# Softmax left undivided in two branches of a decoder trunk: gate over sum, spread by TensorE, multiplied into the head's output

## The reference, cut to what matters

```python
p2 = jax.nn.softmax(s2.reshape(B, Qb, Hk, G, n_top * NSA_SEL_LEN), axis=-1).reshape(s2.shape)
o_s = jnp.einsum('bqhgnl,bqhnld->bqhgd', p2.astype(vsel.dtype), vsel)
...
o_w = banded_attention(q, k_w, v_w, pos, NSA_WINDOW, slopes)
return gates[..., 0:1] * o_c + gates[..., 1:2] * o_s + gates[..., 2:3] * o_w
```

## Time and profile before

| | |
|---|---|
| median of 3 runs | 2594.37 us (2593.79 to 2594.88) |
| the profiled execution's own time | 2596.74 us |
| its span | 2594.9 us |
| PE busy | 94% of the span |
| DVE busy | 59% |
| ACT busy | 44% |
| granted TensorE clock over the span | 0.971 |

### The profile page before, as it was taken

How to read it: one execution, slowest core, us unless ns; L and a number is a source line. 1 busy time by engine, 2 the same in 40 slices (tenths; PEclk the granted TensorE clock), 3 DMA queues, 4 the chain that set the end, 5 groups by cost and what they waited for, 6 DMA issues and landing times.

```text
span 2594.9 us, 37597 instructions
## 1 busy us (share of the span) xinstructions
PE 2437.7 (94%) x13276; PEld 2007.8 (77%) x13276; DVE 1518.7 (59%) x3235; ACT 1136.4 (44%) x2267; POOL 135.0 (5%) x194
## 2 busy tenths in 40 slices
PE   6998899999999889999989998999999988999998
PEld 4887787788877678888868877878878776788886
DVE  5668776772775555552275786767447566455422
ACT  4456564643544532222243564646346445222222
POOL 3000000000002100000010000000000112000000
PEclk8999999999999889999999999999999989999999
DMA  4321122123124113333322211221321420233332
GB/s 110 98 90 34 50 62 61 58 65 97 42 89 123 30 53 96 95 95 95 87 74 74 82 33 57 66 66 50 81 74 50 130 65 25 81 97 97 94 97 69
DMA packets 343959, 193.96 MB, mean 75 GB/s; under 512 B 29825, under 2 KB 339206, under 8 KB 343174
## 3 DMA queue, kind: packets, MB, share of 16 engines
q1 hardware_dynamic: 340512, 178.02, 24.0%
q0 software_dynamic: 2224, 13.67, 1.5%
q10 hardware_dynamic: 1078, 0.36, 0.1%
HBM read 184.69 MB, written 7.34 MB: 74 GB/s over the span
## 4 chain that ended last, share of the span: by engine, by line
PE 81%; DVE 10%; ACT 4%; issue 4%; POOL 1%; DVEq 0%; POOLq 0%; ACTq 0%
PE acc L1257 63%; PE o_acc L1257 5%; PE turn L1461 3%; PE scores L1257 3%; ACT w_hi L797 2%; DVE w_lo L1788 1%; PE turn L1257 1%; DVE ring L2065 1%; PE scores L1446 1%; DVE ring L1873 1%; DVE p_lo L1906 1%; PE scores L1447 1%; DVE trunk L1879 1%; PE scores L1506 1%; PE scores L1325 1%
## 5 line engine op out<-in xcount | busy, mean ns | idle before, releaser
L1788 DVE TENSOR_TENSOR w_lo<-w_f,w_hi 128x1024 fp32r<-128x1024 f32 x336 | 412.0, 1226 | 563.4 <-ACT w_hi L797 563.1
L1257 PE MATMUL acc<-h_hi,w_hi 128*128 128x512 f32 x1680 | 670.7, 399 | 21.3 <-DVE w_lo L1788 9.3
L1257 PE MATMUL acc<-h_lo,w_hi 128*128 128x512 f32 x1680 | 664.7, 396 | 0.0
L1257 PE MATMUL acc<-h_hi,w_lo 128*128 128x512 f32 x1680 | 663.9, 395 | 0.0
L797 ACT ACTIVATE w_hi<-w_f 128x1024 fp32r<-128x1024 f32 x336 | 353.8, 1053 | 295.7 <-PE acc L1257 268.3
L1257 PEld LDWEIGHTS acc<-h_hi,w_hi 128*128 128x128 f32 x1680 | 321.1, 191 | 85.7 <-DVE w_lo L1788 11.0
L1257 PEld LDWEIGHTS acc<-h_hi,w_lo 128*128 128x128 f32 x1680 | 320.4, 191 | 66.8
L1257 PEld LDWEIGHTS acc<-h_lo,w_hi 128*128 128x128 f32 x1680 | 321.2, 191 | 59.8
L853 ACT ACTIVATE p_hi<-turn 128x128 fp32r<-128x128 f32 (+3 forms) x356 | 149.6, 420 | 270.7 <-PE turn L1461 268.5
L1906 DVE TENSOR_TENSOR p_lo<-turn,p_hi 128x128 fp32r<-128x128 f32 (+3 forms) x356 | 165.7, 466 | 73.2 <-ACT p_hi L853 72.6
L941 ACT ACTIVATE ring<-ring,neg_max 128x128 f32<-128x128 f32 (+2 forms) x352 | 188.9, 537 | 38.0 <-DVE neg_max L2065 37.2
(11 more groups left out here) (351 smaller groups left out, 3844.5 us busy)
## 6 DMA issues: line engine op xcount, KB each, us to landing
w_f<-in_ffn_w_in_dram SPq DMA_DIRECT2D x88, 512.0 KB, 3.8
w_f<-in_w_gate_dram SPq DMA_DIRECT2D x64, 512.0 KB, 4.0
w_f<-in_w_in_dram SPq DMA_DIRECT2D x62, 512.0 KB, 3.9
w_f<-in_w_branch_dram SPq DMA_DIRECT2D x32, 512.0 KB, 3.4
w_f<-in_ffn_w_out_dram SPq DMA_DIRECT2D x32, 512.0 KB, 4.0
w_f<-in_w_out_dram SPq DMA_DIRECT2D x16, 512.0 KB, 4.2
w_f<-in_ffn_w_out_dram SPq DMA_DIRECT2D x16, 384.0 KB, 3.4
x_spill<-trunk POOLq DMA_DIRECT2D x2, 2048.0 KB, 6.8
```

The costliest lines, as they stand in the source:

```text
L1257: ins = nc.tensor.matmul(dst, a, b, start=(n == 0 and not added), stop=(n == count - 1))
L1788: nc.vector.tensor_tensor(w_lo[:, u % 2, :], w_f32[:, u % 2, :], w_hi[:, u % 2, :].bitcast(F32), ALU.subtract).then_inc(w_ready, 1)
```

## The change

The exp results of SEL and WIN are turned and multiplied with the values as they are. Once a head, when its four row sums are there, DVE makes gate/sum for the 4x128 queries and splits it (`head_scale`, four instructions on 128x4). PE spreads it over 64 partitions with 8 matmuls against the identity (`spread_scale`), into one more use of the `turn` banks. ACT copies that bank to `square_sum` (`scale_rows`). DVE multiplies `o_acc` with it into `pair_next` (`head_scaled`) and adds the product to `y_nsa` (`out`, one turn of the loop later than before). The other passes keep their division.

```diff
-TURNS = [("v_cmp", 1), ("cmp", 2), ("v_sel", 1), ("sel", 32), ("v_win", 1), ("win", 32),
+TURNS = [("v_cmp", 1), ("cmp", 2), ("v_sel", 1), ("sel", 40), ("v_win", 1), ("win", 40),
...
+    def slot(self, s):
+        return s + max((s - 2) // NT, 0) * (self.gate is not None)
+    def spread_slot(self, h):
+        return min(5 * h + 6, 5 * self.heads - 1)
...
# ScalarE
+                def scale_rows(h):
+                    at = ps.spread_slot(h)
+                    turn_high_part(l, ps.name, 0, at, square_sum[h % 2 * HD:(h % 2 + 1) * HD, :],
+                                   turn[(TB[ps.name] + at) % 2][0:HD, :])
...
+                    if ps.gate is not None and 6 <= s and s % NT == 2:
+                        scale_rows(s // NT - 1)
...
-                    late = 8 if ps is WIN else 6
+                    late = 9 if ps is WIN else 6
...
# TensorE
                 def turn_probs(s):
-                    pe.wait_ge(divided, st + (s + 1))
+                    if ps.gate is None:
+                        pe.wait_ge(divided, st + (s + 1))
+                    else:
+                        wait_apart(pe, exped, st + (s + 1))
...
+                def spread_scale(h):
+                    bank = turn_bank(l, ps.name, 0, ps.spread_slot(h))
+                    pe.wait_ge(gate_split, (2 * l + (ps is WIN)) * H + h + 1)
+                    for i in range(NT):
+                        for m, part in enumerate((gate_hi, gate_lo)):
+                            ins = nc.tensor.matmul(bank[0:HD, i * P:(i + 1) * P],
+                                                   part[:, h % 2, i:i + 1].to_broadcast([P, HD]), ident_r[:, :],
+                                                   start=(m == 0), stop=(m == 1))
+                    ins.then_inc(turned, 1)
...
+                    if ps.gate is not None and s >= 6 and s % NT == 2:
+                        spread_scale(s // NT - 1)
+                if ps.gate is not None:
+                    spread_scale(ps.heads - 1)
...
# VectorE
-                    dve.wait_ge(turned, l * NTN + (TB[ps.name] + max(s - RING + CREDIT, 0) + 1))
+                    free = ps.slot(s - RING) + CREDIT if s >= RING else max(s - RING + CREDIT, 0)
+                    dve.wait_ge(turned, l * NTN + (TB[ps.name] + free + 1))
...
+                def head_scale(h):
+                    done = (2 * l + (ps is WIN)) * H + h + 1
+                    own = gate_over[:, h % 2, :]
+                    dve.wait_ge(exped, st + (4 * h + 4))
+                    nc.vector.reciprocal(over_sum[:, :], row_sum[:, h % 2 * NT:(h % 2 + 1) * NT]).then_inc(inverted, 1)
+                    dve.wait_ge(inverted, st + (h + 1))
+                    nc.vector.tensor_tensor(own, over_sum[:, :], coef[:, ps.gate, :, h], ALU.mult).then_inc(over_gated, 1)
+                    dve.wait_ge(over_gated, done)
+                    nc.vector.tensor_copy(gate_hi[:, h % 2, :], own).then_inc(gate_high, 1)
+                    dve.wait_ge(gate_high, done)
+                    nc.vector.tensor_tensor(gate_lo[:, h % 2, :], own, gate_hi[:, h % 2, :].bitcast(F32),
+                                            ALU.subtract).then_inc(gate_split, 1)
+                def head_scaled(h):
+                    rows, t = slice(h % 2 * HD, (h % 2 + 1) * HD), TB[ps.name] + ps.spread_slot(h)
+                    dve.wait_ge(turn_high, l * NTN + (t + 1))
+                    dve.wait_ge(applied, st + (4 * h + 6))
+                    dve.wait_ge(head_done, l * NHD + (HB[ps.name] + h + 1))
+                    nc.vector.tensor_tensor(pair_next[rows, :], o_acc[h % 2][0:HD, :], square_sum[rows, :],
+                                            ALU.mult).then_inc(turn_ready, 1)
...
                 def out(h):
-                    dve.wait_ge(applied, st + (4 * h + 6))
+                    dve.wait_ge(turn_ready, l * NTN + (TB[ps.name] + ps.spread_slot(h) + 3))
-                    nc.vector.tensor_tensor(dst, src, dst, ALU.add).then_inc(head_done, 1)
+                    nc.vector.tensor_tensor(dst, pair_next[rows, :], dst, ALU.add).then_inc(head_done, 1)
...
                     if 1 <= s <= ps.steps:
-                        divide(s - 1)
+                        if ps.gate is None:
+                            divide(s - 1)
+                        elif s % NT == 0:
+                            head_scale(s // NT - 1)
...
-                    if s >= 7 and (s - 7) % 4 == 0 and (s - 7) // 4 < ps.heads:
-                        out((s - 7) // 4)
-                    if ps is WIN and s >= 13 and (s - 13) % 8 == 0:
-                        nsa_rest((s - 13) // 8)
+                    if ps.gate is not None and s >= 7 and (s - 7) % 4 == 0 and (s - 7) // 4 < ps.heads:
+                        head_scaled((s - 7) // 4)
+                    late = 7 if ps.gate is None else 8
+                    if s >= late and (s - late) % 4 == 0 and (s - late) // 4 < ps.heads:
+                        out((s - late) // 4)
+                    if ps is WIN and s >= 14 and (s - 14) % 8 == 0:
+                        nsa_rest((s - 14) // 8)
```

More of the change, by code:

```diff
@@ L286, in build @@
         neg_max = sb("neg_max", [P, 4])
-        row_sum = sb("row_sum", [P, 4])
+        row_sum = sb("row_sum", [P, 8])
+        gate_over = sb("gate_over", [P, 2, NT])
+        gate_hi = sb("gate_hi", [P, 2, NT], F32R)
+        gate_lo = sb("gate_lo", [P, 2, NT], F32R)
         sink_exp = sb("sink_exp", [P, 4])
@@ L384, in build @@
         divided = sem("divided")
+        over_gated = sem("over_gated")
+        gate_high = sem("gate_high")
+        gate_split = sem("gate_split")
         out_high = sem("out_high")
@@ L934, in probabilities @@
                 def probabilities(s):
+                    many = 4 if ps.gate is None else 8
                     h, i = divmod(s, NT)
@@ L949, in high @@
                         act.wait_ge(cmp_applied, 2 * KVH * (l + 1))
-                    turn_high_part(l, ps.name, 0, s, p_hi[0:rows, s % 2, 0:n * P],
-                                   turn[(TB[ps.name] + s) % 2][0:rows, 0:n * P])
+                    at = ps.slot(s)
+                    turn_high_part(l, ps.name, 0, at, p_hi[0:rows, s % 2, 0:n * P],
+                                   turn[(TB[ps.name] + at) % 2][0:rows, 0:n * P])
+                def scale_rows(h):
+                    at = ps.spread_slot(h)
+                    turn_high_part(l, ps.name, 0, at, square_sum[h % 2 * HD:(h % 2 + 1) * HD, :],
+                                   turn[(TB[ps.name] + at) % 2][0:HD, :])
                 def out_high_part(h):
@@ L1457, in turn_probs @@
                     n, w = ps.tiles(s % NT)
-                    bank = turn_bank(l, ps.name, 0, s)
-                    pe.wait_ge(divided, st + (s + 1))
+                    bank = turn_bank(l, ps.name, 0, ps.slot(s))
+                    if ps.gate is None:
+                        pe.wait_ge(divided, st + (s + 1))
+                    else:
+                        wait_apart(pe, exped, st + (s + 1))
                     for t in range(n):
@@ L1473, in apply @@
                         pe.wait_ge(cmp_out, 2 * KVH * (l + 1))
-                    pe.wait_ge(turn_ready, l * NTN + (TB[ps.name] + s + 3))
+                    pe.wait_ge(turn_ready, l * NTN + (TB[ps.name] + ps.slot(s) + 3))
                     for t in range(n):
@@ L2082, in divide @@
                     p = ring[:, s % RING, 0:ps.keys(i)[1]]
-                    if ps.gate is None:
-                        nc.vector.tensor_scalar(p, p, over_sum[:, c], None, ALU.mult).then_inc(divided, 1)
-                    else:
-                        nc.vector.tensor_scalar(p, p, over_sum[:, c], coef[:, ps.gate, i, h:h + 1], ALU.mult,
-                                                ALU.mult).then_inc(divided, 1)
+                    nc.vector.tensor_scalar(p, p, over_sum[:, c], None, ALU.mult).then_inc(divided, 1)
+                def head_scale(h):
[17 more added lines that the diff above has]
+                                            ALU.mult).then_inc(turn_ready, 1)
                 def out(h):
@@ L2117, in attend @@
                     value_turns(l, *values)
-                for s in range(ps.steps + 6):
+                for s in range(ps.steps + (6 if ps.gate is None else 7)):
                     if s < ps.steps:
@@ L2125, in attend @@
                         n, rows = ps.tiles(t % NT)
-                        turn_rest(l, ps.name, 0, t, p_lo[0:rows, t % 2, 0:n * P],
-                                  turn[(TB[ps.name] + t) % 2][0:rows, 0:n * P], p_hi[0:rows, t % 2, 0:n * P])
+                        at = ps.slot(t)
+                        turn_rest(l, ps.name, 0, at, p_lo[0:rows, t % 2, 0:n * P],
+                                  turn[(TB[ps.name] + at) % 2][0:rows, 0:n * P], p_hi[0:rows, t % 2, 0:n * P])
                     for n, (name, k) in enumerate(ps.filler):
@@ L2133, in attend @@
                             stage(n)
-                    if s >= 7 and (s - 7) % 4 == 0 and (s - 7) // 4 < ps.heads:
```

(8 more changed lines are left out.)

2 lines of the change are left out of this document (1 added, 1 removed).

## The result

The changed kernel takes 2618.2 us (median of 4 runs, 2617.45 to 2619.61), the kernel before 2594.62 us in the same session (4 runs, 2593.79 to 2600.55). The ratio is 1.0087, with a 95% interval of 1.0072 to 1.0101: slower by 0.9%, 23.6 us. The prediction said 2615 and 2601 to 2627.

What follows compares the result with a forecast made beforehand. PE was taken as the bound. A layer: SEL 2.85, SEL to WIN 2.7, WIN 2.65, behind WIN 1.4, clock 0.75, together 10.35; two layers +20.7 on 2594.4, about 2615 us, range 2601 to 2627.

Steps and rivals of the forecast that it cites:

- The sum by periods: Inside SEL and WIN: split and plain periods grow, the first period gains; +2.85 in SEL, +2.65 in WIN a layer.
- WIN's last period: End of WIN's pass: the last head's spread falls before the filler ends and adds 0.48 us.
- the price of the earlier trace: Spread on PE: upper bound from a 128-wide scale's spread, 0.14 us a matmul, 1.1 us a head, 36 us.
- The 81 ns of the Trainium skill: Spread on PE: about 81 ns a matmul would make 0.65 us a head, 5 us more over the kernel.
- The boundary: From SEL to WIN: last spread and ACT's copy precede WIN's weight split; PE stands 3.6 us or more; +2.7.
- The end of WIN: Behind WIN: ACT's copy and `head_scaled` join the chain to `y_lo`, latency 1.65, tail shorter by 0.6; +1.4 to 1.5.
- The clock: Start of WIN: PE's stand may drop it to 1.2 GHz, losing up to 1.7 us; one in two, 0.75 a layer.
- the rival in which VectorE's relief wins: SEL, WIN and tails: DVE was the bound, stalls go, 11 us a layer; less 15.4 for the spread, 2588 us; 7%.
- the 0.35 of the prediction: Last turns of SEL, without filler: the last values product ends 0.35 us earlier than before.
- gains and spread cancel: Rival, SEL and WIN: split periods lose their stall (-9.8), the tails keep half of theirs: 2597 us; 9%.
- ACT's copy delays the exp: SEL and WIN: the copy's 0.59 us a head lies in ACT's idle time; otherwise exps late, stall grows as much.

Runs made afterwards that it cites:

- WIN's keys first: Changed kernel with SEL's last head finished (copy, product, add) behind WIN's first weight split and keys: 2611.66 us, ratio 1.0057.
- the double spread: Changed kernel with sixteen spread matmuls a head instead of eight, the same values computed twice: 2633.07 us, ratio 1.0129.
- the run with the later add: Changed kernel with the head's output add and what follows it one more turn later, no longer between `w_lo` and the bias: 2608.94 us, ratio 1.0042.
- both moves: Changed kernel with output add one turn later and SEL's last head finished behind WIN's keys: 2599.07 us, ratio 1.0010.
- the last kernel: Changed kernel with output add later, SEL's last head behind WIN's keys, spread as four turns, last spread ahead of last values product: 2595.1 us, ratio 0.9998.
- half the spread: Changed kernel with four spread matmuls a head instead of eight, low part of gate over sum left out: 2613.84 us, ratio 1.0054.
- the kernel with both moves and the last spread early: Changed kernel with add later, SEL's last head behind WIN's keys, each pass's last spread ahead of its last values product: 2602.83 us, ratio 1.0017.

## Why the prediction was right

The forecast was 2615 us, +20.7; measured 2618.2, +23.6, and +20.2 in the stages that the change touches. Slower was given 0.84.

*The sum by periods held in SEL, and in WIN only with the clock's help.* SEL +2.85 and WIN +2.65 a layer were forecast; +2.81 and +2.92 were measured between the first and last bias. But WIN's 2.92 holds the low clock, which the forecast counted by itself: with the clock at 1.00 (WIN's keys first) WIN takes 59.10 us, +1.5. The single periods came at 8.58 and 9.15 to 9.42 (forecast 8.55 and 9.2) in SEL and 7.71 and 8.7 (7.6 and 8.9) in WIN; too much was forecast above all for WIN's last period, to which 0.48 was added and which did not grow (7.81 us between the bias rows of 512 keys before, 7.71 after). The spread's 0.48 us a head was right (0.059 a matmul), and the double spread shows that each further matmul counts whole; the price of the earlier trace rows was not paid. The 81 ns of the Trainium skill (TensorE: Matmul & The Clock Gate, Back-to-back issue gap) is not what this stream took.

*The boundary held:* first scores behind 3.72 and 3.70 us of standing (3.6 forecast). The stage grew by 2.44 for 2.7. *The end of WIN* was too small in the sum: the wait came (1.80 us), and the stage grew by 2.0 for 1.4. *The clock* was given one in two and fell in both layers; it costs 1.3 to 1.4 us a layer by the runs, for 0.75 in the sum. So the 10.35 a layer against 10.1 measured is partly luck: WIN 1.1 too much and the boundary 0.3, the clock and the end of WIN 0.6 too little each.

*What VectorE gives and takes was mis-sized on both sides, and the total hides it.* I let the missing division give back 0.3 to 0.45 in a split period and little elsewhere, and so put the removal at 6 to 7 us a layer when it went to the test. It was worth 8.8, against the 11 of the rival in which VectorE's relief wins. Between the ends of `p_lo` of 512 keys, split periods of WIN went from 8.35 to 7.70 and plain ones from 7.26 to 7.08; in SEL the split ones from 8.85 to 8.38, and the plain ones not at all (7.79 to 7.77), as forecast. Most of the rest came at the ends of the passes, which have no filler: SEL's last period gave 0.8 to 1.1, WIN's 1.4, and the boundary 1.3, for the 0.35 of the prediction. What took it away again is the other half of VectorE's exchange, 6.9 us a layer for four small operations, product and add. I had priced the add at 0.6 in each of six split periods, 3.6 a layer, and that is what these periods show; the 3.3 in WIN's plain periods, in the last period of each pass and at the end of WIN were not in the sum. The exchange leaves 1.9 us a layer of gain, for VectorE's 22.7 us less of busy time.

*The sum of the causes,* a layer: the divisions gone -8.8; VectorE's new work +6.9; spread, copy and clock +12.0, of which the issue of 128 spread matmuls is 7.7. The run with the double spread shows the 7.7 for the second eight; for the first eight the periods of SEL and the timeline show the same price. The other 4.3 lie at the ends and in the clock: the boundary (9.42 to 13.11, 2.7 beyond the 0.96 of its two spreads), the end of WIN (36.31 to 37.89, 0.6 beyond its two) and WIN (56.58 to 60.53, 1.1 beyond its six). That is +10.1. This is one order of adding the parts up, and the parts are not independent: with the add one turn later SEL's split periods are as long as its plain ones, with the spread in them.

*The rivals.* That the relief wins failed not for lack of a stall but because its new operations stand at worse places than the old ones: the place of the add alone is 3 to 4 us a layer, as the run with the later add shows, some 2.9 of it in the split periods. That gains and spread cancel became nearly true only with both moves made (2.8 to 2.9 us a layer short by the stages). That ACT's copy delays the exp and so the loop is not seen: the stall behind `w_lo` went with the copy in place, and SEL's periods grow by the matmuls alone.

What stays open: how the 2.7 us at the boundary divide between the copy, the late product and the order behind them. No run kept the matmuls and dropped the copy; finishing the last head behind the keys gave 1.8 of them back.

## What to carry to other kernels

Where TensorE issues all the time, work moved to it was paid whole here, by the pitch of its matmuls (0.06 us), while work taken off the other engine was paid back only where that engine was waited for; and the place of a new instruction in that engine's order can cost more than its length (0.6 us of add, 3 to 4 us a layer until it stood one turn later). Instructions of the last item of a pass that stand ahead of the next pass's first loads are worth looking at first: two moves in the order gave back 7.3 of the 10.1 us a layer, and no arithmetic was changed. Price the removal and each addition by a kernel that has only that: a right total can hold errors that cancel, as it did here.

## What I had not expected of the hardware

The clock moves the time outside the edit. In the changed kernel's layer 0, around 850 us, where both kernels run the same code, the granted clock was low for 10.2 us; before, it was low for 3.4 us at the same place. The stretches, after first, then before:

```profile
843.90:854.10 10.20, 9.57 (x27) 7.83 (x28) 10.07 (x13) 6.30 (x10) 3.42 (x2) 0.50 0.11 40
```

```profile
835.30:838.70 3.40, 3.08 (x7) 2.48 (x8) 3.40 (x5) 2.24 (x4) 1.71 (x1) 0.50 0.20 75
838.70:845.50 6.80, 6.80 (x39) 5.84 (x38) 6.67 (x9) 3.85 (x6) 1.72 (x1) 1.00 0.01 2
```

The way from the last FOX bias to the first XA bias was 118.8 us before and 121.8 after (in layer 1 121.7 and 121.8), and from 117.4 to 122.2 in the other kernels, without regard to the edit. The start went the other way: SEL's first bias came 2.05 us earlier in the changed kernel (159.35 for 161.40), ahead of any edit. Summed over stretches of 5 us, the clock was low for 154 us of the span before, 171 after, 151 with both moves, and 181 in the profiled execution of the last kernel, which took 2611.5 us where the median of its 13 runs is 2595.1. The start of WIN shows it too. PE stood 3.7 us there in the changed kernel, in the one with half the spread and in the one with the later add, and the clock was then low for 3.4, 6.8 (both layers) and 6.8 or 3.4 us (layer 0, layer 1). And in the kernel with both moves and the last spread early PE stood 1.13 and 1.38 us in layer 0, 1.14 and 1.38 in layer 1; the clock fell in layer 0 alone:

```profile
235.90:239.30 3.40, 3.40 (x10) 2.52 (x9) 2.36 (x8) 1.47 (x5) 0.00 (x0) 0.50 0.45 119
1511.86:1515.26 3.40, 3.34 (x20) 2.55 (x19) 2.58 (x9) 2.08 (x7) 0.00 (x0) 1.00 0.44 114
```

So one such stand does not say whether the clock falls, and WIN's keys first did not make its fall impossible. A change of 0.2% in this kernel is therefore better read from the stages that it touches than from the total.
